# The first attention block of a two-block transformer kernel: query tiles in alternating order, and one gate tile moved into the fill

## The reference, cut to what matters

```python
h = rms_norm(x, norm_g) * (1.0 + scale) + shift
proj = h @ w_in
ssm_u, ssm_z, q, k, v, attn_z, q_idx, k_idx, w_idx = split(proj)
y_ssm = s5_mixer(ssm_u, ...) * silu(ssm_z)              # ends in a gated product with w_glu
# in dsa_mixer: score picks the top-k keys of each query (causal)
logits = q @ k_sel * scale + rel_bias[bucket]
logits = where(dist >= 0, logits, -inf)
y_attn = (softmax(logits) @ v_sel) * silu(attn_z)
x = x + gate * (concatenate([y_ssm, y_attn]) @ w_out)
```

## Time and profile before

| what | value |
| --- | --- |
| median of 3 runs | 1301.26 us |
| the profiled execution's own time | 1303.57 us |
| its span in the profile | 1301.8 us |
| TensorE busy | 1274.4 us, 98% |
| VectorE busy | 937.8 us, 72% |
| ScalarE busy | 383.4 us, 29% |
| GpSimd busy | 272.8 us, 21% |
| the attention stage, from the end of the `az` matmuls to the row product after the last unit | 287.7 to 348.9 us |

### The profile page before, as it was taken

One profiled execution on the slowest core, in us unless ns is written; L12 is line 12 of the kernel. 1 busy time (PEld: TensorE's weight loads), 2 busy tenths in 40 slices (PEclk: granted clock), 3 DMA queues, 4 the chain that ended last, 5 costly groups with the idle time before them and its releaser, 6 DMA issues.

```text
span 1301.8 us, 17512 instructions
## 1 busy us (share of the span) xinstructions
PE 1274.4 (98%) x6240; PEld 916.7 (70%) x6240; DVE 937.8 (72%) x2143; ACT 383.4 (29%) x951; POOL 272.8 (21%) x260
## 2 busy tenths in 40 slices
PE   4999999999999999999999999999999999999998
PEld 3544455544788886885455557888888888888887
DVE  5898999868786797655456776766877777686563
ACT  4223221216511103323456674110232232320000
POOL 1158587305103568700000000001000000000000
PEclk9999999999999999999999999999999999999999
DMA  9792433651412123202120003123232232233210
GB/s 321 196 158 90 135 84 94 178 210 61 157 45 80 65 93 102 98 1 98 65 48 19 1 2 66 65 88 92 65 98 96 66 109 85 65 123 121 96 42 33
DMA packets 91041, 120.67 MB, mean 93 GB/s; under 512 B 16488, under 2 KB 52654, under 8 KB 90956
## 3 DMA queue, kind: packets, MB, share of 16 engines
q1 hardware_dynamic: 86256, 110.81, 28.2%
q10 hardware_dynamic: 2956, 5.05, 1.2%
q0 software_dynamic: 1744, 3.70, 1.0%
HBM read 111.00 MB, written 6.84 MB: 91 GB/s over the span
## 4 chain that ended last, share of the span: by engine, by line
PE 96%; ACT 2%; DVE 1%; issue 0%; DMA 0%; ACTq 0%; DVEq 0%
PE bank L1578 19%; PE bank L1604 10%; PE bank L930 10%; PE bank L1240 9%; PE bank L917 8%; PE bank L1506 7%; PE bank L1464 6%; PE bank L952 6%; PE bank L1344 4%; PE bank L1416 3%; PE bank L1444 3%; PE bank L981 2%; PE bank L1549 2%; PE bank L1196 1%; PE bank L1087 1%; PE bank L1175 1%
## 5 line engine op out<-in xcount | busy, mean ns | idle before, releaser
L1578 PE MATMUL bank<-arena 128*128 128x256 f32 x1120 | 241.9, 379 | 0.0
L1578 PEld LDWEIGHTS bank<-arena 128*128 128x128 f32 x1120 | 212.8, 190 | 28.9
L1604 PE MATMUL bank<-arena 128*128 128x256 f32 x616 | 133.1, 379 | 0.0
L1604 PEld LDWEIGHTS bank<-arena 128*128 128x128 f32 x616 | 117.0, 190 | 15.9
L930 PE MATMUL bank<-arena 128*128 128x512 f32 x288 | 127.7, 596 | 0.0
L952 PEld LDWEIGHTS bank<-arena 128*128 128x128 f32 (+2 forms) x644 | 77.1, 145 | 68.2 <-issue 45.7
L1240 PE MATMUL bank<-arena 128*128 128x256 f32 x560 | 122.4, 380 | 0.0
L1240 PEld LDWEIGHTS bank<-arena 128*128 128x128 f32 x560 | 106.0, 190 | 15.1 <-issue 0.7
L952 PE MATMUL bank<-arena 128*128 128x128 f32 (+2 forms) x644 | 91.7, 281 | 18.9 <-ACT arena L1688 7.3
L3164 DVE CUSTOM_DVE_ANT_0 arena<-bank,arena 128x128 f32<-128x128 f32 (+3 forms) x128 | 57.5, 488 | 66.1 <-PE bank L1416 64.4
L917 PE MATMUL bank<-arena 128*128 128x512 f32 (+1 forms) x256 | 102.2, 552 | 0.0
(11 more groups left out here) (400 smaller groups left out, 2006.7 us busy)
## 6 DMA issues: line engine op xcount, KB each, us to landing
arena<-in_w_in SPq DMA_DIRECT2D x14, 2048.0 KB, 7.8
arena<-in_w_up SPq DMA_DIRECT2D x20, 1024.0 KB, 7.0
arena<-in_w_ada SPq DMA_DIRECT2D x16, 512.0 KB, 9.1
arena<-in_w_down SPq DMA_DIRECT2D x8, 1024.0 KB, 7.3
arena<-in_w_out SPq DMA_DIRECT2D x2, 2048.0 KB, 9.3
arena<-in_w_attn_br SPq DMA_DIRECT2D x8, 512.0 KB, 7.7
arena<-in_w_o SPq DMA_DIRECT2D x2, 2048.0 KB, 7.9
rb_dram<-rb_one_dram ACTq DMA_DIRECT2D x1, 2560.0 KB
```

The costliest lines, as they stand in the source:

```text
L1578: mm = pe.matmul(ps, left[:, k, :], right[:, k, :], start=(first and k == 0), stop=(k == 3), skip_group_check=True)
L1604: mm = pe.matmul(down_acc(i, name), left, right, start=first and name in ("P1", "P7", "P2", "P4"), stop=last, skip_group_check=True)
```

## The change

The order of the units becomes: tiles 1 and 0 in turn for the four pairs of heads, then tiles 3 and 2 in turn. `az` tile 3 leaves the projections and becomes the first fill tile, eight matmuls, four in each of the first two rounds; it is computed in bank 7. `FILL1_TO` now sums to 26. On GpSimd and VectorE the mask buffers are counted by masked units (`MASKED1`), as these are not the last twelve any more. VectorE reads `az` tile 3 out in the round after the one in which it ends, ahead of a `gate` tile.

```diff
-        name_proj(*four("u"), "ki", *four("qi"), *four("k"), *four("v"), *four("q"), *four("z"), *four("az"))
+        name_proj(*four("u"), "ki", *four("qi"), *four("k"), *four("v"), *four("q"), *four("z"), *four("az")[:3])
...
-        SUB1 = [(i, p) for i in range(TT) for p in range(4)]
+        SUB1 = [(i, p) for q in range(2) for p in range(4) for i in (2 * q + 1, 2 * q)]
+        MASKED1 = [n for n, (i, p) in enumerate(SUB1) if i]
...
-        FILL1_TILES = [("gate", 0), ("gate", 1)] + four("glu")
+        FILL1_TILES = [("az", 3), ("gate", 0), ("gate", 1)] + four("glu")
...
-        FILL1_TO = [1, 2, 2, 2, 4, 6, 8, 10, 12, 13, 14, 16, 17, 18, 18, 18]
+        FILL1_TO = [4, 8, 9, 10, 10, 12, 14, 16, 18, 20, 22, 23, 24, 25, 26, 26]
...
+        chunk("az", ("fill", ("az", 3)), KT, 512, [(0, 512, lambda: cols_of(w_in, 0, KT, 2560, 3072))])
...
-            proj_cols("az", "az", hT)
+            for j in range(3):
+                one_cols("az", j, "az", hT)
...
                     for kind, j in fill1_ends(n):
+                        if kind == "az":
+                            fill_ready(act, ("az", j))
+                            act.activation(az[:, j, :], fbank(("az", j))[:, :], ACT.Tanh, scale=0.5).then_inc(az_tanh, 1)
...
                 if i:
+                    r = MASKED1.index(n)
                     for e in range(2):
-                        if n >= 2:
-                            pool.wait_ge(lg_done, 2 * (n - 2) + e + 1)
-                        pool.tensor_tensor(mb[:, n % 2, e, 0:cols], biasT[:, 2 * p + e, 128 * (3 - i):512],
+                        if r >= 2:
+                            pool.wait_ge(lg_done, 2 * MASKED1[r - 2] + e + 1)
+                        pool.tensor_tensor(mb[:, r % 2, e, 0:cols], biasT[:, 2 * p + e, 128 * (3 - i):512],
...
             def fill1(kind, j):
+                if kind == "az":
+                    v.wait_ge(az_tanh, j + 1)
+                    v.scalar_tensor_tensor(az[:, j, :], az[:, j, :], 1.0, fbank(("az", j))[:, :], ALU.add, ALU.mult)\
+                        .then_inc(ffree(("az", j)), 1)
+                    return
...
+                for kind, j in fill1_ends(n - 1) if 0 < n <= NS1 else ():
+                    if kind in ("az", "glu"):
+                        fill1(kind, j)
                 for kind, j in fill1_ends(n) if n < NS1 else ():
                     if kind == "gate":
-                        fill1(kind, j)
-                for kind, j in fill1_ends(n - 1) if 0 < n <= NS1 else ():
-                    if kind == "glu":
                         fill1(kind, j)
```

More of the change, by code:

```diff
@@ L308, in program @@
                 name_aux(("pv", n - 3), banks=6)
-        FILL1_TILES = [("gate", 0), ("gate", 1)] + four("glu")
+        FILL1_TILES = [("az", 3), ("gate", 0), ("gate", 1)] + four("glu")
         name_fill(*FILL1_TILES)
-        FILL1_MM = [(key, k) for key in FILL1_TILES for k in range(4 if key[0] == "glu" else 1)]
-        FILL1_TO = [1, 2, 2, 2, 4, 6, 8, 10, 12, 13, 14, 16, 17, 18, 18, 18]
+        FILL1_MM = [(key, k) for key in FILL1_TILES for k in range({"az": KT, "gate": 1, "glu": 4}[key[0]])]
+        FILL1_TO = [4, 8, 9, 10, 10, 12, 14, 16, 18, 20, 22, 23, 24, 25, 26, 26]
         assert len(FILL1_TO) == NS1 and FILL1_TO[-1] == len(FILL1_MM)
@@ L501, in program @@
         w1chunk("qi", ("qi", 3), 3072)
-        for name, c0 in (("k", 1536), ("v", 2048), ("q", 1024), ("z", 512), ("az", 2560)):
+        for name, c0 in (("k", 1536), ("v", 2048), ("q", 1024), ("z", 512)):
             w1chunk(name, (name, 3), c0)
+        chunk("az", ("fill", ("az", 3)), KT, 512, [(0, 512, lambda: cols_of(w_in, 0, KT, 2560, 3072))])
         chunk(("gate", 0), ("gsum", 1), KT, 512, [(0, 512, lambda: cols_of(w_ada, 0, KT, 2048, 2560))])
@@ L1154, in pair_scores @@
                     for h in range(2):
-                        mm = pe.matmul(score_bank(n, e, ("az", 3))[64 * h:64 * h + 64, 0:128 * (i + 1)],
+                        mm = pe.matmul(score_bank(n, e, ("az", 2))[64 * h:64 * h + 64, 0:128 * (i + 1)],
                                        qT[r, p, 128 * i + 64 * h:128 * i + 64 * h + 64],
@@ L1191, in pair_fill @@
                     else:
-                        w = weights(pe, "glu")
+                        w, right = weights(pe, kind), {"az": hT, "glu": zz}[kind]
                         kt = w.shape[1]
-                        if k == 0:
+                        if k == 0 and kind == "glu":
                             pe.wait_ge(z_done, TT)
-                        mm = pe.matmul(fbank(key)[:, :], w[:, k, 128 * j:128 * j + 128], zz[:, k, :],
+                        mm = pe.matmul(fbank(key)[:, :], w[:, k, 128 * j:128 * j + 128], right[:, k, :],
                                        start=(k == 0), stop=(k == kt - 1))
@@ L1247, in _ @@
                 if n < 2:
-                    first = 2 * ((n + (PBANK["az", 3] < 2)) % 2)
+                    first = 2 * ((n + (PBANK["az", 2] < 2)) % 2)
                     for b in (first, first + 1):
@@ L1869, in _ @@
             az_in(2)
-            az_in(3)
             def pair_exp(n):
@@ L2748, in pair_logits @@
                     if i:
-                        v.wait_ge(mb_done, 2 * (n - 4) + e + 1)
-                        bias = mb[:, n % 2, e, 0:cols]
+                        r = MASKED1.index(n)
+                        v.wait_ge(mb_done, 2 * r + e + 1)
+                        bias = mb[:, r % 2, e, 0:cols]
                     else:
@@ L2753, in pair_logits @@
                     c0 = 16 + 2 * (n % 2) + e
-                    v.tensor_tensor_reduce(pr[:, n % 3, e, 0:cols], score_bank(n, e, ("az", 3))[:, 0:cols], bias,
+                    v.tensor_tensor_reduce(pr[:, n % 3, e, 0:cols], score_bank(n, e, ("az", 2))[:, 0:cols], bias,
                                            -1.0, 3.0e38, ALU.add, ALU.min, sml[:, c0:c0 + 1]).then_inc(lg_done, 1)
```

## The result

| | before | changed |
| --- | --- | --- |
| median | 1301.26 us (5 runs, 1300.29 to 1303.74) | 1305.96 us (5 runs, 1304.67 to 1307.45) |
| ratio, 95% interval | | 1.0029 (1.0017 to 1.0042) |
| the profiled execution, its span | 1303.57, 1301.8 us | 1305.96, 1304.2 us |
| from unit 0's scores to the row product after the last unit, with az tile 3 in it | 68.06 us | 69.76 us |

The change is slower by 4.7 us by the medians, 0.3%, where I had forecast +0.3 us. In the last line az tile 3 is in both: before it is 348.90 - 287.72 = 61.18 us, and 6.88 us (8 x 0.86) for the tile ahead of it; after it is 351.31 - 281.55.

The account below looks back on a forecast made before the run. TensorE, busy nearly throughout, was taken to bound the kernel. Groups +0.2, the stage's waits -3.58, gate wait +2.2 and glu waits +1.5 gave +0.3 us on 1301.26: 1301.6 us, range 1300.1 to 1303.4.

Parts of the forecast that it names:

- What bounds the kernel: Whole kernel: TensorE is busy 1274.4 of 1301.8 us; the edited stage holds only 3.69 us of idle time to win.
- Moved work costs nothing: Az tile 3, eight matmuls or 6.9 us, leaves the place ahead of the units and returns as fill at no cost.
- More groups: Fill in the attention stage: 14 rounds filled where 12 were, costing +0.2 us.
- The waits that go: TensorE waits before unit 1's transposes (1.39 us), unit 13's transposes (0.68 us) and the second gate matmul (0.57 us) vanish.
- The wait that comes: Before the first gate matmul TensorE waits 2.2 us (1.9 to 2.5) for VectorE to read az tile 3 from bank 7.
- The glu tiles: Three TensorE waits for bank 7 before glu matmuls, together 1.5 us (0.9 to 2.6), against 0.94 us before.
- The weights of the output projection: Second w_out half loads after the last glu matmul in round 14: 7.7 us, covered by 9.8 us of TensorE work.
- The rival of the clock: The clock falls to half in the new gate wait: 1.7 us slower, time 1303.3 us; chance 0.15.
- The rival of alternation: Alternating wide and narrow units lets ScalarE catch up, glu waits vanish: -1.5 us, 1300.1 us; chance 0.15.

Follow-up runs that it names:

- e1: The changed kernel again with no edit: median 1306.06 us against 1303.13 us for the kernel before, ratio 1.0026.
- e7: Changed kernel with az tile 3 back among the projections and the old fill table: median 1303.64 us, ratio 1.0007 to the kernel before; stage 1.11 us longer.
- the 35: 35 further executions of the kernel before, unedited, on each of two chips: medians 1303.13 and 1303.26 us.
- e4: Changed kernel with every glu fill matmul one round earlier and az tile 3 in bank 6: median 1302.04 us, ratio 0.9993 to the kernel before.
- e8: Changed kernel with az tile 3 in bank 6 and a fill table leaving out rounds where ScalarE is behind: median 1300.36 us, ratio 0.9982 to the kernel before.
- e5: Changed kernel with two extra 512-column matmuls in each of its two new waits (before first gate matmul and first row product): median 1303.47 us.

## Why the prediction was wrong

- **What bounds the kernel**: right. The difference is idle time or clock of TensorE in the stage, and scatter ahead of it.
- **Moved work costs nothing**: right. Behind the stage every trace takes 952.9 us.
- **More groups**, +0.2 us: not found. The stage is 1.70 us longer and the idle times in brackets are 1.73 us more.
- **The waits that go**: right, all three of them: no wait before unit 1's or unit 13's transposes nor before the second gate matmul.
- **The wait that comes**: 2.2 us were given and 2.01 measured. The chain is as walked; the logits start at 290.48, the scaling takes 0.43 us where I took 0.5, the product starts at 291.73. The upper end, with the scaling at 0.84 us, did not come: GpSimd's sums were running from 291.00 us, and the scaling still took 0.43 us. (With the scaling at 0.29 us the chain adds up to 2.0 us, not the 1.9 of the text.)

```profile
290.48 0.42 DVE L2765 CUSTOM_DVE_ANT_0 arena<-bank,arena 128x256 f32<-128x256 f32 x1 [2.99 <-PE bank L1158]
...
291.37 0.43 DVE L2776 TENSOR_SCALAR arena<-arena 128x128 f32<-128x128 f32 x1
291.73 0.67 DVE L2733 SCALAR_TENSOR_TENSOR arena<-arena,bank 128x512 f32<-128x512 f32 x1
```

- **The glu tiles**, 0.37 + 0.26 + 0.86 = 1.5 us: measured 0.42 + 0.22 + 0.88 = 1.52. (4.8 less 3.97 is 0.83, not 0.86; it changes nothing.)
- **The weights of the output projection**: this is the first step that failed. I followed the late last glu matmul to the load that it releases, which landed in time (7.8 us from its issue at 333.54), and not to the row product's other input, the glu tile itself. The chain tanh, round 15's logits and scaling, L2743, L2744 ends 1.78 us after TensorE is ready. With it the sum would have been +2.1 us, against the 1.7 us of the stage, and the forecast 1303.4 us, at the very end of the range. What lies beyond it is the clock and the base.
- **The rival of the clock** is the second step: its mechanism was right, and its price of 1.7 us for a fall near the 1.6 us by which each lengthened the stage. I gave it 0.15 for one wait, on the ground that 1.39 us had not brought a fall. It is 3 in 5 for a wait of 2.0 us, and there were two such waits. The fall at 27 us, which I quoted, followed a wait of only 1.32 us, so the trace of before had one fall behind two waits shorter than the new one, and I did not let that move the chance. The Trainium skill (TensorE: Matmul & The Clock Gate, Part 1) has the array go back to 1.2 GHz after idling. The falls behind the two waits in e1 agree with it in kind (granted clock 0.50 behind 2.00 and 1.78 us); that the fall at 58 us came behind no idle time does not follow from it.
- **The rival of alternation** was wrong in sign: e7 has +1.1 us for it.
- **The base**: the median of the first runs lies 1.9 us below that of 35. That was luck, and it is the largest single part of the 4.7 us: against the 35 the changed kernel is slower by 2.9 us in the medians. A kernel whose executions scatter like this needs more than five of them: its 35 run from 1300.3 to 1306.0.

## What to carry to other kernels

When a step is moved later, list every wait on its semaphore in the program, and not only the one that its weights are behind: here the same event released a load and, through two more engines, an operand. Where TensorE is near 100% busy at the full clock, a wait of 2 us can cost more than 2 us: break it up (e4, e8 with no wait over 1.2 and 0.8 us) or fill it with matmuls (e5), and price it with the fall. Where one bank passes from tile to tile, the first read-out stands behind whatever the reading engine does first in its round; another bank that is idle then, as bank 6 here, removes the wait with one line.

## What the runs showed of the hardware that was not expected

A fall of the clock lost 1.7 us of work each time, at 27, 293 and 340 us; the one at 57 to 67 us lost 3.4, twice that. In time it cost less: 1.6 us each in the stage, and 2.9 us at 57 to 67 us (17.41 against 14.55 us for the same work, in all four traces that have it). In the stage, waits of 1.39 us (three traces), 1.42 and 1.59 us (one trace each) were not followed by one, waits of 2.01 and 1.78 us in three of five each; at 25 us a wait of 1.32 us was, in seven of fourteen; and the fall at 57 to 67 us followed no wait at all. With four matmuls that nobody reads in the two new waits the mean clock was 0.9995, against 0.9972 without them, of which a part lies ahead of the stage. In some executions a fall also stands in the last 2 us, behind the last matmul, where it costs nothing but lowers the mean clock shown by 0.0007.
